# Splitting turned attention probabilities straight from PSUM, on ScalarE and VectorE alone

## The reference

```
def sparse_attend(q, k_sel, v_sel, valid):
    ...
    logits = jnp.einsum('bqngd,bqsnd->bqngs', qg, k_sel).astype(jnp.float32) * (HEAD_DIM ** -0.5)
    logits = jnp.where(valid[:, :, None, None, :], logits, -jnp.inf)
    p = jax.nn.softmax(logits, axis=-1).astype(v_sel.dtype)
    o = jnp.einsum('bqngs,bqsnd->bqngd', p, v_sel)
```

## Time and profile before

| | us |
|---|---|
| median of 3 runs | 2116.79 (2115.79 to 2118.52) |
| the profiled execution's own time | 2117.71 |
| its span, first to last instruction | 2115.9 |
| PE busy | 1929.0 (91%) |
| DVE busy | 1115.5 (53%) |
| POOL busy | 686.3 (32%) |
| ACT busy | 513.2 (24%) |

### The profile page before, as it was taken

The page is one execution under the profiler, slowest core; times in us unless marked ns, Lnnn a source line. Parts: engine busy times, 40 slices in busy tenths (PEclk is TensorE's granted clock), DMA queues, the critical chain, the costliest instruction groups (busy, mean ns, idle before and its releaser), DMA issues. The chain is left out here.

```text
span 2115.9 us, 28957 instructions
## 1 busy us (share of the span) xinstructions
PE 1929.0 (91%) x11623; PEld 1781.0 (84%) x11623; DVE 1115.5 (53%) x1924; ACT 513.2 (24%) x725; POOL 686.3 (32%) x430
## 2 busy tenths in 40 slices
PE   4887999999999398888886999999999999999997
PEld 3753899999999255655665999999999999999997
DVE  3353767799978757545342433533433344334335
ACT  3242011112111245434232232211111111111114
POOL 0407133222221345534322621433333333233330
PEclk7958999999999679889675999999999999999998
DMA  6105111132320043322211721111111111111102
GB/s 231 36 7 159 50 51 31 56 92 72 90 76 1 23 158 118 123 80 80 81 30 37 258 76 30 60 44 46 40 50 40 50 40 50 40 43 47 40 14 83
DMA packets 130170, 144.34 MB, mean 68 GB/s; under 512 B 15725, under 2 KB 110285, under 8 KB 129669
## 3 DMA queue, kind: packets, MB, share of 16 engines
q1 hardware_dynamic: 113192, 77.29, 12.7%
q0 software_dynamic: 11920, 46.35, 6.6%
q10 hardware_dynamic: 4978, 19.59, 2.5%
HBM read 123.74 MB, written 19.13 MB: 68 GB/s over the span
## 5 line engine op out<-in xcount | busy, mean ns | idle before, releaser
L226 PE MATMUL ps<-act_hi,w_hi 128*128 128x358 f32 (+1 forms) x1080 | 243.4, 334 | 13.1 <-POOL act_lo L458 7.8
L542 POOL TENSOR_TENSOR w_lo<-w_raw,w_hi 128x1024 fp32r<-128x1024 f32 (+1 forms) x57 | 139.8, 2457 | 306.1 <-ACT w_hi L537 299.9
L226 PE MATMUL ps<-act_hi,w_lo 128*128 128x358 f32 (+1 forms) x1080 | 238.9, 329 | 0.0
L226 PE MATMUL ps<-act_lo,w_hi 128*128 128x358 f32 (+1 forms) x1080 | 238.8, 330 | 0.0
L226 PE MATMUL ps<-x_gain_hi,w_hi 128*128 128x358 f32 x1056 | 231.4, 327 | 0.0
L226 PE MATMUL ps<-x_gain_hi,w_lo 128*128 128x358 f32 x1056 | 231.2, 327 | 0.0
L226 PE MATMUL ps<-x_gain_lo,w_hi 128*128 128x358 f32 x1056 | 230.6, 326 | 0.0
L1036 DVE TENSOR_SCALAR_CACHE_REDUCE count_junk<-scores,candidate 128x384 uint8<-128x384 f32 (+6 forms) x217 | 200.9, 990 | 0.0
L226 PEld LDWEIGHTS ps<-act_hi,w_hi 128*128 128x128 f32 (+1 forms) x1080 | 186.6, 191 | 15.0 <-issue 11.3
L226 PEld LDWEIGHTS ps<-act_lo,w_hi 128*128 128x128 f32 (+1 forms) x1080 | 188.0, 190 | 1.0
L226 PEld LDWEIGHTS ps<-act_hi,w_lo 128*128 128x128 f32 (+1 forms) x1080 | 188.0, 190 | 1.0
(11 more groups left out here) (374 smaller groups left out, 3562.1 us busy)
## 6 DMA issues: line engine op xcount, KB each, us to landing
w_raw<-in_ffn_up SPq DMA_DIRECT2D x44, 512.0 KB, 3.9
w_raw<-in_w_in SPq DMA_DIRECT2D x32, 512.0 KB, 3.8
w_raw<-in_ffn_down SPq DMA_DIRECT2D x12, 512.0 KB, 3.4
w_odd_raw<-in_ffn_down SPq DMA_DIRECT2D x10, 512.0 KB, 3.5
x_save<-xt SPq DMA_DIRECT2D x1, 4296.0 KB, 12.8
mix_b<-row ACTq DMA_DIRECT2D x8, 537.0 KB, 3.4
sig_a<-row ACTq DMA_DIRECT2D x8, 537.0 KB, 2.9
sig_a_in<-sig_a ACTq DMA_DIRECT2D x8, 537.0 KB, 4.1
```

Of the source, the lines that this page charges most:

```text
L226: last = pe.matmul(core.acc(out_set)[0:rows, c, :], w(k), b(k)[:, c * CH:(c + 1) * CH], start=(k == 0 and n == 0), stop=(k == kblocks - 1 ...
L542: eng.tensor_tensor(self.core.wl[slot][:, 0:width], self.core.wr[slot][:, 0:width], self.core.wh[slot][:, 0:width].bitcast(F32), ALU.subtr ...
```

## The change

C is gone. H reads the piece from PSUM and has C's wait on `turned`, with its guard on `valued`. Lo is now on DVE, in the place where C stood, reads the piece from PSUM and H's result from SBUF, and has POOL's wait on `hi`. PE's wait ahead of a turn is on `lo` in place of `t_copied`. POOL keeps only the gathers.

```
-                after(pe, t_copied, before[j] + x)
+                after(pe, lo, before[j] + x)
...
             def high(j, x):
-                act.wait_ge(t_copied, before[j] + x + 1)
-                _, p_hi, _, p_raw = piece(j, x)
-                act.activation(p_hi, p_raw, ACT.Copy).then_inc(hi, 1)
+                pair = j // 2
+                act.wait_ge(turned, before[j] + x + 1)
+                after(act, valued, FULL if pair in (FULL, FULL + 1) else pair - 1)
+                src, p_hi, _ = piece(j, x)
+                act.activation(p_hi, src, ACT.Copy).then_inc(hi, 1)
...
-            def low(j, x):
-                pool.wait_ge(hi, before[j] + x + 1)
-                _, p_hi, p_lo, p_raw = piece(j, x)
-                pool.tensor_tensor(p_lo, p_raw, p_hi.bitcast(F32), ALU.subtract).then_inc(lo, 1)
...
-                j = turning(i)
-                if j >= 0:
-                    for x in range(len(pieces(j))):
-                        low(j, x)
...
-            def copy(j, x):
-                pair = j // 2
-                dve.wait_ge(turned, before[j] + x + 1)
-                after(dve, valued, FULL if pair in (FULL, FULL + 1) else pair - 1)
-                src, _, _, p_raw = piece(j, x)
-                dve.tensor_copy(p_raw, src).then_inc(t_copied, 1)
+            def low(j, x):
+                dve.wait_ge(hi, before[j] + x + 1)
+                src, p_hi, p_lo = piece(j, x)
+                dve.tensor_tensor(p_lo, src, p_hi.bitcast(F32), ALU.subtract).then_inc(lo, 1)
...
-                    copy(j, 0)
+                    low(j, 0)
...
-                    copy(j, 1)
+                    low(j, 1)
```

More of the change, by code:

```diff
@@ L1584, in attention_stage @@
           for x in range(2)]
-    pr = [nc.alloc_sbuf_tensor_at(f"probs_turned{x}", [128, NT, 2, 128], F32, offset=Map.W + 2 * wide * x + wide)
-          for x in range(2)]
     slim = NT * 2 * 16 * 4
@@ L1590, in attention_stage @@
     lpl = [nc.alloc_sbuf_tensor_at(f"last_turned_lo{x}", [128, NT, 2, 16], F32R, offset=at + 2 * slim * x + slim)
-           for x in range(2)]
-    lpr = [nc.alloc_sbuf_tensor_at(f"last_turned{x}", [128, NT, 2, 16], F32, offset=at + 2 * slim * x + slim)
            for x in range(2)]
@@ L1603, in attention_stage @@
     logits, masked, exped, normed = sem("logits"), sem("masked"), sem("exped"), sem("normed")
-    inverted, turned, t_copied, hi, lo = sem("inverted"), sem("turned"), sem("t_copied"), sem("hi"), sem("lo")
+    inverted, turned, hi, lo = sem("inverted"), sem("turned"), sem("hi"), sem("lo")
     valued, r_ok, padded, split_hi = sem("valued"), sem("r_ok"), sem("padded"), sem("split_hi")
@@ L1637, in piece @@
         where = (slice(0, rows), slice(tiles[0], tiles[-1] + 1), j % 2, slice(0, n))
-        three = (ph, pl, pr) if qb < NT - 1 else (lph, lpl, lpr)
-        return (src, *(t[pair % 2][where] for t in three))
+        halves = (ph, pl) if qb < NT - 1 else (lph, lpl)
+        return (src, *(t[pair % 2][where] for t in halves))
     def turning(i):
```

## The result

| | before | changed |
|---|---|---|
| median, us | 2116.55 (4 runs) | 2165.93 (2163.37 to 2171.09, 4 runs) |
| span of the profiled execution | 2115.9 | 2163.6 |
| PE busy in it | 1929.0 | 1950.6 |
| POOL busy in it | 686.3 | 583.2 |

The ratio is 1.0235, with a 95% interval of 1.0215 to 1.0255: 49 us slower. The forecast was 2157, with a range of 2134 to 2180.

What follows compares the result with a forecast made beforehand. PE, busy for 91% of the span, was taken as the bound. Terms 1 to 4, 13.6 + 14 + 4 + 9 = 40.6 us on 2117.71, gave 2158.3, predicted as 2157 for the median; range 2134 to 2180.

Steps and rivals of the forecast that it cites:

- term 2: Blocks 5 and 6: PE's ten waits for item copies each 1.4 us longer, DVE's copy held behind Lo; 14 us.
- term 4: Attention stage: longer PE pauses let the granted clock fall, 1.7 us each at half of ten pauses; 9 us.
- What is cheaper or equal: Lo on DVE takes 0.69 us, H from PSUM 591 ns, at 512 columns; POOL loses some 100 us.
- Term 1: Blocks 4 to 8: bank 4 freed only after Lo, so PE waits ahead of turns; 9 plus 4.6, together 13.6 us.
- Term 3: Small delays: later M in one-piece steps (blocks 0 to 3), the samples' exponential waiting for DVE, and others; 4 us.
- the relief of DVE from POOL: Blocks 1 to 4: N on DVE quicker without POOL's load; if DVE is waited for, 2096 us; chance 0.06.

## Why the prediction was right, and what it mis-sized

The sign, the mechanism and the time (2157 for 2166) held. That the time came so near owes something to luck: as PE's idle and busy time show them, term 2 was put too high and term 4 too low, and the two errors offset each other.

- **What is cheaper or equal**: right. Lo took 692 ns for 690, H 592 for 591. POOL lost 103 us of work and no run shows a gain from it.
- **Term 1, bank 4 late, 13.6 us**: right in mechanism and at the places named (T0 3.86 us behind M for 3.91; blocks 7 and 8 together 9.3 us more for 8.5, though block 7 had the higher clock now, 0.79 for 0.74). It was too small in all: PE's waits at turns grew by 19.2 us, and with the late bank alone PE also waited in block 3 (twice, 2.6 us), which I had taken as hidden under the logits. The experiment with the late bank alone, which frees it even 0.8 us sooner, cost 20.
- **Term 2, the held copy, 14 us**: right in mechanism (1.4 us in the step shown) and confirmed by both moves that take the hold away, H1 ahead of E and Lo1 behind the item. As idle time of PE it shows as less: the ten pauses grew from 17.7 to 25.1 us, for the first item of a step ran longer at the low clock (1.91 us for 1.04 in the step shown) and filled part of the pause.
- **Term 3, 4 us**: the step that failed. Blocks 1 to 3 lost 7.9, and 6.0 of them in block 3 (35.6 us for 29.6). The missed piece is the samples' exponential there, 3.74 us on ACT: H0 stood behind it, Lo0 behind H0, and PE waited 3.9 us for bank 4 (the longest wait above), where C had needed nothing of ACT. Moving the exponential took that wait away and gave back 1.8 us, and block 3 still took 34.2. The late bank alone cost 4.5 in block 3, and holding DVE with bank 4 early cost 16 in blocks 1 to 3, so each is able to cost there by itself; how the 7.9 divide stays open. The old scheme in these blocks removes all of it.
- **Term 4, the clock, 9 us**: too small. PE's busy time for the same instructions in blocks 5 and 6 grew by 17.6 us. With the 7.4 of the pauses this makes 25 us, where terms 2 and 4 had 23 together. The prediction took pauses of up to 2.4 us to leave the clock alone. The trace of the kernel before says otherwise: in block 6 the clock was 0.50 behind a pause of 2.04 us of PE (the row below), so this kernel already paid for its short pauses, as the fill in it confirms.
- **The rivals**: the relief of DVE from POOL is real (N 576 for 1236 ns) and brought no net gain, as the kernel with Lo late on DVE shows, though DVE does more there too. No run shows its condition, that DVE be what is waited for.

The window behind that pause of 2.04 us, which ended at 961.61 in the kernel before:

```profile
961.60:964.60 3.00, 2.99 (x14) 2.99 (x15) 0.69 (x1) 0.60 (x1) 1.16 (x2) 0.50 0.00 0
```

## What to carry to other kernels

Cheaper instructions can make a dearer kernel when they tie two engines' queues together: DVE now waited in the middle of its queue for ACT, which waited in its queue for DVE. Before moving an operation, write down what it waits for and what stands ahead of that on the other engine; here a swap of two lines on ACT was worth 44 us, and the 112 instructions fewer bought nothing. Where PE pauses for 2 to 3 us again and again, look at the granted clock as well as at the idle time, and try idle work in the pause.

## What the runs showed of the hardware

- Twelve useless multiplications in each of the pauses of 0.8 to 3.1 us ahead of second items made the kernel before 16 us faster; the granted clock of block 7 went from 0.74 to 1.00, though PE had 109 instructions more there.
- A subtraction with one operand in PSUM costs what a copy from PSUM does (692 and 688 ns for 512 columns). A multiplication by a column of scalars in SBUF took 1236 ns for 640 columns, as the mean of 8, where POOL subtracted in the same stretch, and 576 without. The mean hides single ones from 0.55 to 2.41 us: the one at 846.99 took 1.51, beside a subtraction of POOL from 846.87 to 848.13.
- Pauses of PE of 2 us can already be followed by the low clock (0.50 behind one of 2.04). With the pauses of block 6 filled, its clock went from 0.92 to 1.00.
